# Differential attention: the first turn of a unit between the halves of its second scores, and six value tiles in front of them instead of three

## The chip, the cores and the metric

One core of a Trainium2 chip runs the whole kernel. The metric is the time of one execution on the device in microseconds; of the kernel before, three runs and one profiled execution are known. The clock of TensorE (PE) is told as granted clock, 1.00 being 2.4 GHz and 0.50 being 1.2 GHz.

## What is computed

The reference is two blocks of a model over 2048 positions with 1024 channels, in float32. The change concerns one part of the first block, the differential attention with 4 heads. Each head has two sets of queries and keys (64 wide) and one set of values (128 wide):

```python
def block(args):
    qblk, qp = args
    s = jnp.einsum('bqhce,bkhce->bchqk', qblk, k).astype(jnp.float32) * scale
    dist = jnp.abs(qp[:, None] - pos[None, :]).astype(jnp.float32)
    s = s - slopes[:, None, None] * dist
    a = jax.nn.softmax(s, axis=-1)
    w = a[:, 0] - lam * a[:, 1]
    return jnp.einsum('bhqk,bkhe->bqhe', w.astype(v.dtype), v)
```

## The kernel before, in words

The stage `diff_attention` works through 64 units, 4 heads by 16 tiles of 128 queries. A unit's scores against all 2048 keys are made twice (set s = 0 and s = 1), turned into weights, mixed, transposed ("turned") and multiplied with the values. Everything is held in order by semaphores, and each engine's instructions stand in an order written out by hand, one loop over m for each engine. The waits are placed as `wait_ge` in front of an instruction, and an engine does not pass over a waiting instruction.

Names used below, with what each waits for:

- S00, S01, S10, S11 are the calls `scores(m + 2, s, half)` of PE (L2033), s first, half second. Each fills two of the four banks `score` with 1024 keys: three passes of two matmuls. Half 0 has banks 0 and 1, half 1 banks 2 and 3. A call waits until DVE has read the scores that its banks held before (`score_read[half]`), so S11 waits for B01 of the same unit, and S10 for B00.
- B00, B01, B10, B11 are `bias_and_top(m + 2, s, half)` of DVE (L1974): they add the distance term, write the result into `e` and keep the running minimum (`half_top`, then `neg_top`). B01 and B11 are over when the accumulator has been read.
- E0 and E1 are `exp(m + 2, s)` of ACT (L1894). E0 needs B01's minimum, E1 needs B11's. Both leave a sum.
- The reciprocal (L1984, `invert_total(m + 1)`) needs the sum of E1 of the turn before. The mix (L1994, `mix(m + 1)`) combines both sets of weights.
- T0 and T1 are `transposes(m, group)` of PE (L2044), 16 small matmuls each, into the two banks `turn`. T0 needs the mix of unit m and, like T1, that ACT has moved what the banks held before.
- Moves are `move(m, r)` of ACT (L1902), two for each turn, from `turn` to `w_t`.
- V-first and V-rest are `values(m - 1, first, last)` of PE (L2061): 16 value tiles of 128 keys, each with 2 calls, which the trace shows as 4 matmuls. V-first is tiles 0 to EARLY - 1, V-rest is EARLY to 15. They add into the two banks `out`, which have no second buffer; V-first waits for `a_copied`, that is for C of the unit before (m - 2). V-rest tells `valued` at its end.
- C is `copy_out(m - 2)` of ACT (L1909): it needs `valued` of unit m - 2 and moves `out` to `a_parts`. POOL adds the two parts (L1851), ACT squares the sum (L1916), and SP stores it (L1818).

The order of one turn of the loop, for m in the middle, on each engine:

```
PE   S00 S01 V-first T0 S10 S11 V-rest T1
DVE  B00 reciprocal B01 B10 weigh B11 mix
ACT  C, moves of T1 (unit m-1), moves of T0 (unit m), E0, square, E1
```

POOL also makes the high and low parts of later queries and keys, and pieces of a bias table for the stage behind; SP loads queries, keys and values. Neither is touched.

Of the kernel before, what the change touches and what calls it, by code (L numbers as in the profile page):

```python
# [1694 lines left out]
def diff_attention(nc, c, inputs, wait_z_stored, lambdas, cols, rows, a_rows, a_sums, a_squares, bias):  # L1695
# [7 lines left out]
    UNITS = DIFF_HEADS * NT  # L1703

    with Phase(nc, "d") as ph:
# [52 lines left out]
        def wait_q_made(eng, n):  # L1758

            if n == 0:  # L1760
                eng.wait_ge(q_first_made, 1)
            else:
                eng.wait_ge(q_made, n)

        def wait_k_made(eng, h, s):

            if h == 0:
                eng.wait_ge(k_first_made, s + 1)
            else:
                eng.wait_ge(k_made, 2 * h)  # L1770

        EARLY = 3
        FILLED_AT = (11, 12, 15)

        def quad_of(m):

            return m // 4

        def wait_mixed(eng, m, group):

            if group == 0:
                eng.wait_ge(mixed, m + 1)

        def wait_turn_free(eng, m, group):

            if 2 * m + group >= 1:
                eng.wait_ge(moved, 4 * m + 2 * group)

        def wait_group_moved(eng, m, group):

            eng.wait_ge(moved, 4 * m + 2 * group + 2)

        @block.sync
        def _(sp):
            def load_v(h):
                at = (DV + h) * P
                sp.dma_start(v[:, h % 2], rows[:, at:at + VW].rearrange("(t p) n -> p t n", p=P))\
                  .then_inc(v_loaded[h % 2], 16)

            for n, vec in enumerate(lambdas):  # L1800
                sp.dma_start(lam_in[:, n], row_on_all(vec, P)).then_inc(lam_loaded, 16)
            load_v(0)
            load_v(1)
            wait_z_stored(sp)
            bias.load_first(sp, cols)
            for m in range(UNITS):
                h, t = m // NT, m % NT
                if m % 4 == 0 and quad_of(m) + 2 < DIFF_HEADS * QUADS:
                    wait_q_made(sp, quad_of(m))
                    inputs.load_q(sp, quad_of(m) + 2)  # L1810
                if t == 1 and h + 1 < DIFF_HEADS:
                    wait_k_made(sp, h, 1)
                    inputs.load_k(sp, h + 1)
                if t == 3 and 1 <= h and h + 1 < DIFF_HEADS:
                    sp.wait_ge(valued, NT * h)
                    load_v(h + 1)
                sp.wait_ge(a_added, m + 1)
                sp.dma_start(a_rows[t * P:(t + 1) * P, h * VW:(h + 1) * VW], a_out[:, m % 4]).then_inc(a_stored[m % 4], 16)  # L1818
            for s in range(4):
                sp.wait_ge(a_stored[s], 16 * UNITS // 4)  # L1820
# [197 lines left out]
        @block.tensor  # L2018
        def _(pe):
            def scores(m, s, half):  # L2020
                h, n = m // NT, quad_of(m)
                if m % 4 == 0 and s == 0 and half == 0:
                    wait_q_made(pe, n)
                if m % NT == 0 and half == 0:
                    wait_k_made(pe, h, s)
                if 2 * m + s >= 1:
                    pe.wait_ge(score_read[half], 2 * m + s)
                queries = slice((m % 4) * P, (m % 4 + 1) * P)
                keys = slice(half * BANK, (half + 1) * BANK)
                for n_pass, (q_part, k_part) in enumerate(((q_hi, k_hi), (q_hi, k_lo), (q_lo, k_hi))):  # L2030
                    for b in range(2):
                        at = slice(b * HD, (b + 1) * HD)
                        mm = pe.matmul(score[:, 2 * half + b], q_part[at, n % 2, s, queries], k_part[at, h % 2, s, keys],  # L2033
                                       start=(n_pass == 0), stop=(n_pass == 2))
                mm.then_inc(scored, 1)

            def transposes(m, group):
                wait_mixed(pe, m, group)
                wait_turn_free(pe, m, group)
                for b in range(8):  # L2040
                    kt = 8 * group + b
                    for side in range(2):
                        at = slice(side * HD, (side + 1) * HD)
                        mm = pe.transpose(turn[:, side, b * HD:(b + 1) * HD], e[at, m % 3, 0, kt * P:(kt + 1) * P],  # L2044
                                          ident[at, at])
                mm.then_inc(turned, 1)

            def values(m, first, last):
                h = m // NT
                if first == 0:  # L2050
                    if m % NT == 0:
                        pe.wait_ge(v_loaded[h % 2], 16 * (h // 2 + 1))
                    if m >= 1:
                        pe.wait_ge(a_copied, m)
                    wait_group_moved(pe, m, 0)
                for kt in range(first, last):
                    if kt == 8:
                        wait_group_moved(pe, m, 1)
                    for side in range(2):
                        at = slice(side * HD, (side + 1) * HD)  # L2060
                        mm = pe.matmul(out[:, side, 0:VW], w_t[at, m % 2, kt], v[at, h % 2, kt], start=(kt == 0),  # L2061
                                       stop=(kt == NT - 1))
                if last == NT:
                    mm.then_inc(valued, 1)

            for m in range(-2, UNITS + 1):
                if m + 2 < UNITS:
                    scores(m + 2, 0, 0)
                    scores(m + 2, 0, 1)
                if m >= 1:  # L2070
                    values(m - 1, 0, EARLY)
                if 0 <= m < UNITS:
                    transposes(m, 0)
                if m + 2 < UNITS:
                    scores(m + 2, 1, 0)
                    scores(m + 2, 1, 1)
                if m >= 1:
                    values(m - 1, EARLY, NT)
                if 0 <= m < UNITS:
                    transposes(m, 1)  # L2080
# [1672 lines left out]
def build(nc, a, choice, result):  # L3753
# [14 lines left out]
    with Phase(nc, "k") as ph:  # L3768
# [14 lines left out]
        with Phase(nc, "b") as held:  # L3783
            bias = DilatedBias(held, c["carry"])
            diff_attention(nc, c, diff_inputs, wait_z_stored, [a[f"lambda_{n}"] for n in ("q1", "k1", "q2", "k2")], cols, rows, a_rows, a_sums,
                           a_squares, bias)
            dilated_attention(nc, c, cols, rows, o_parts, bias, w_merge, a_sums, a_squares, root)
            held.clear()
# [35 lines left out]
```

## Time and profile before

| | |
|---|---|
| median of 3 runs | 2932.22 us (2930.03 to 2933.57) |
| profiled execution | 2932.87 us, its span 2931.0 us, mean granted clock 0.972 |
| busy share of the span | PE 93%, DVE 70%, ACT 53%, POOL 36% |
| the stage | scores from 766.4 us, last values from 1295.3 us |
| one turn of its loop | 8.05 us |

The page gives the busy time of each engine, waits with the instruction that ended them ("<-"), and groups of instructions by line. A matmul's length in the trace is partly modelled and overlaps with the next, so PE's cost is read from start to start. "x12" means that twelve instructions of one kind in a row are merged into one line, and the number in front is then the length of them all.

### The profile page before, as it was taken

How to read it: one execution, taken by the hardware profiler on the slowest of the kernel's cores; microseconds unless marked ns; L12 is line 12 of the kernel's file. 1: busy time of each engine (PE TensorE's matmuls, PEld its weight loads, DVE VectorE, ACT ScalarE, POOL GpSimd, SP SyncE). 2: the span in 40 equal slices, each digit the busy share in tenths (PEclk: the TensorE clock that was granted, in tenths of full speed). 3: DMA queues.
4: the chain of work that ended last, by engine and by line, in shares of the span. 5: the costliest groups of instructions: out<-in, count | busy, mean ns of one | idle time of the engine just before them, and what ended most of it. 6: DMA issues, size and time to landing. Idle time of an engine off the chain costs nothing. (4 is left out here: it accounts for less than half of the span.)

```text
span 2931.0 us, 54522 instructions
## 1 busy us (share of the span) xinstructions
PE 2731.9 (93%) x21026; PEld 2233.1 (76%) x21026; DVE 2045.2 (70%) x3027; ACT 1559.6 (53%) x3111; POOL 1053.4 (36%) x803
## 2 busy tenths in 40 slices
PE   7899989999699999989998899899899999799998
PEld 5678867888588888878887678688677788577776
DVE  5767687666799999967777765433567767466675
ACT  6574446644588888867776221322433343455553
POOL 4677656776122222129550543200021111221211
PEclk9999999999899999999999899899999999899999
DMA  3433323332412121023443666242165465744441
GB/s 115 129 108 94 94 80 93 108 108 87 133 24 54 32 53 25 24 63 114 119 119 109 235 217 252 85 145 79 51 181 132 98 158 161 177 148 135 144 155 67
DMA packets 317438, 330.11 MB, mean 113 GB/s; under 512 B 24401, under 2 KB 259969, under 8 KB 314113
## 3 DMA queue, kind: packets, MB, share of 16 engines
q1 hardware_dynamic: 287184, 292.59, 32.8%
q0 software_dynamic: 6912, 23.07, 2.7%
q10 hardware_dynamic: 23088, 11.02, 1.6%
q8 instruction: 166, 2.72, 0.4%
q14 instruction: 88, 0.71, 0.1%
HBM read 217.13 MB, written 109.47 MB: 111 GB/s over the span
## 5 line engine op out<-in xcount | busy, mean ns | idle before, releaser
L1049 PE MATMUL p_acc<-p_y_hi,p_x_hi 128*128 128x512 f32 x904 | 362.2, 401 | 11.4 <-DVE p_y_lo L841 3.8
L1049 PE MATMUL p_acc<-p_y_lo,p_x_hi 128*128 128x512 f32 x904 | 356.4, 394 | 0.0
L1049 PE MATMUL p_acc<-p_y_hi,p_x_lo 128*128 128x512 f32 x904 | 356.1, 394 | 0.0
L562 POOL TENSOR_TENSOR p_x_lo<-k_carry,p_x_hi 128x1024 fp32r<-128x1024 f32 x113 | 281.1, 2494 | 131.9 <-ACT p_x_hi L634 131.9
L1894 ACT ACTIVATE d_e<-d_e,d_neg_top 128x2048 f32<-128x2048 f32 x128 | 256.9, 2007 | 18.9 <-DVE d_neg_top L1974 18.9
L2061 PEld LDWEIGHTS d_out<-d_v,d_w_t 64*128 64x128 f32 x4096 | 248.0, 188 | 11.9 <-ACT d_a_parts L1909 0.8
L920 DVE RECIPROCAL p_aux<-p_aux 128x512 f32<-128x512 f32 x64 | 215.1, 3361 | 57.5 <-ACT p_aux L730 57.5
L2061 PE MATMUL d_out<-d_v,d_w_t 64*128 64x128 f32 x4096 | 249.7, 272 | 0.7 <-ACT d_a_parts L1909 0.7
L1565 PE MATMUL s_acc<-s_y_hi,s_x_hi 128*128 128x512 f32 x560 | 224.1, 400 | 22.0 <-DVE s_x_lo L1369 12.9
L1565 PE MATMUL s_acc<-s_y_lo,s_x_hi 128*128 128x512 f32 x560 | 221.5, 395 | 0.0
L1565 PE MATMUL s_acc<-s_y_hi,s_x_lo 128*128 128x512 f32 x560 | 221.1, 395 | 0.0
L1049 PEld LDWEIGHTS p_acc<-p_y_hi,p_x_hi 128*128 128x128 f32 x904 | 172.3, 191 | 50.5 <-issue 9.3
L2327 ACT ACTIVATE l_e<-l_score,l_stage 128x256 f32<-128x256 f32 (+1 forms) x384 | 163.1, 438 | 86.6 <-DVE l_stage L2368 86.5
L1049 PEld LDWEIGHTS p_acc<-p_y_hi,p_x_lo 128*128 128x128 f32 x904 | 171.8, 190 | 37.8
L1049 PEld LDWEIGHTS p_acc<-p_y_lo,p_x_hi 128*128 128x128 f32 x904 | 172.0, 190 | 34.8
L1851 POOL TENSOR_TENSOR d_a_out<-d_a_parts 128x128 f32<-128x128 f32 x64 | 29.5, 460 | 412.7 <-ACT d_a_parts L1909 372.8
L1974 DVE CUSTOM_DVE_ANT_0 d_e<-d_score,d_dist 128x1024 f32<-128x1024 f32 x128 | 156.5, 1222 | 29.6 <-PE d_score L2033 29.6
L1902 ACT ACTIVATE d_w_t<-d_turn 128x512 f32<-128x512 f32 x256 | 138.1, 593 | 68.7 <-PE d_turn L2044 68.5
L1974 DVE CUSTOM_DVE_ANT_0 d_e<-d_score,d_dist,d_half_top 128x1024 f32<-128x1024 f32 x128 | 164.4, 1284 | 6.4
L243 POOL DMA_DIRECT2D k_carry<-in_a_w_in x72 | 53.8, 752 | 311.7 <-DVE s_x_lo L1369 311.3
L3577 DVE CUSTOM_DVE_ANT_0 w_e_in<-w_score,k_carry,w_less 128x256 f32<-128x256 f32 (+1 forms) x256 | 111.4, 473 | 73.0 <-PE w_score L3674 72.3
L634 ACT ACTIVATE p_x_hi<-k_carry 128x1024 fp32r<-128x1024 f32 x113 | 119.2, 1056 | 80.1 <-PE p_acc L1049 56.0
(367 smaller groups left out, 7097.6 us busy)
## 6 DMA issues: line engine op xcount, KB each, us to landing
k_carry<-in_w_in SPq DMA_DIRECT2D x128, 256.0 KB, 3.3
k_carry<-in_a_w_in POOLq DMA_DIRECT2D x72, 256.0 KB, 3.6
cols<-p_z SPq DMA_DIRECT2D x64, 256.0 KB, 2.6
w_q<-q SPq DMA_DIRECT2D x15, 1024.0 KB, 8.2
o_parts<-l_stage SPq DMA_DIRECT2D x192, 66.0 KB, 1.8
m_o<-o_parts SPq DMA_DIRECT2D x48, 264.0 KB, 5.9
k_carry<-cols SPq DMA_DIRECT2D x48, 256.0 KB, 4.7
j_x_second<-x SPq DMA_DIRECT2D x20, 512.0 KB, 3.8
```

The source lines that it names most:

```text
L243: sp.dma_start(self.w_raw[:, j, k_half, c_half], self.w_b[block][:, k_half, c_half]).then_inc(arrived, 16)
L562: pool.tensor_tensor(x_lo[:, m % RING], inputs.place(x_place(m)), x_hi[:, m % RING].bitcast(F32), ALU.subtract).then_inc(x_lo_made, 1)
L634: act.activation(x_hi[:, m % RING], inputs.place(place), ACT.Copy).then_inc(x_hi_made, 1)
L920: dve.reciprocal(norm_bank(m), norm_bank(m)).then_inc(root_inverted, 1)
L1049: mm = pe.matmul(bank_of(n, j), x_part[:, n % RING, j, kt], y_part[:, y_slot(n), kt], start=(kt == 0 and m == 0 and not (g == 0 and n % 2 ...
L1565: mm = pe.matmul(bank_of(n, j), x_part[:, n % RING, j, kt], y_part[:, form, kt], start=(kt == 0 and m == 0), stop=(kt == 3 and m == 2))
L1894: act.activation(e[:, m % 3, s], e[:, m % 3, s], ACT.Exp, bias=neg_top[:, m % 2, s:s + 1], scale=-1.0, accum_out=sums).then_inc(exped, 1)
L1902: act.activation(w_t[:, m % 2, 8 * group:8 * group + 8, side * HD:(side + 1) * HD], turn[:, side].rearrange("p (b n) -> p b n", n=HD), ACT ...
L1974: dve.tensor_tensor_reduce(e[:, m % 3, s, half * HALF:(half + 1) * HALF], score[:, 2 * half:2 * half + 2].rearrange("p a b -> p (a b)"), d ...
L2061: mm = pe.matmul(out[:, side, 0:VW], w_t[at, m % 2, kt], v[at, h % 2, kt], start=(kt == 0), stop=(kt == NT - 1))
L2327: act.activation(e[:, u % 4, h, 0:width(n)], score[:, 2 * (n % 2) + h, scores_of(n, j)], ACT.Exp, bias=stage[:, u % SLOTS, 2 * HD + h:2 * ...
L3577: dve.tensor_tensor_reduce(e_in[:, h, at], score[:, s % 2, j * WIN + at.start:(j + 1) * WIN], tables[:, h, at], -1.0, less[:, h:h + 1], AL ...
```

## The change

V-first takes six value tiles (24 matmuls in the trace) where it took three (12), V-rest takes ten (40) where it took thirteen (52), and T0 stands behind S10 where it stood in front of it. S10 and S11 with T0 between them are the halves of the second scores. The other engines' orders, all waits and all buffers stay. PE's order becomes S00 S01 V-first S10 T0 S11 V-rest T1. In turns without scores (the last three) or without values (the first ones) the calls that exist keep this order.

```diff
-        EARLY = 3
+        EARLY = 6
...
                     scores(m + 2, 0, 1)
                 if m >= 1:
                     values(m - 1, 0, EARLY)
+                if m + 2 < UNITS:
+                    scores(m + 2, 1, 0)
                 if 0 <= m < UNITS:
                     transposes(m, 0)
                 if m + 2 < UNITS:
-                    scores(m + 2, 1, 0)
                     scores(m + 2, 1, 1)
                 if m >= 1:
                     values(m - 1, EARLY, NT)
```

## Rows read from the trace of the kernel before

**Rows 1.** Busy time by engine in one stretch of the stage, with the granted clock

```profile
1100.00:1200.00 100.00, 96.05 (x1510) 85.54 (x1508) 93.12 (x138) 84.11 (x137) 25.13 (x34) 1.00 0.11 26
```

**Rows 2.** Who waited for whom, from 1000 to 1250 us: total, times, longest

```profile
ACT d_w_t L1902 <- PE d_turn L2044: 33.6, 31, 1.1
...
DVE d_e L1974 <- PE d_score L2033: 15.2, 32, 0.5
PE d_score L2033 <- DVE d_neg_top L1974: 10.2, 31, 0.3
```

**Rows 3.** PE in order of time over one turn of the loop: start, length, count

```profile
1207.33 0.66 PE L2044 MATMUL d_turn<-k_ident,d_e 64*128 64x64 f32 x16
1207.79 0.48 PE L2033 MATMUL d_score<-d_k_hi,d_q_hi 64*128 64x512 f32 x2
...
1208.58 0.39 PE L2033 MATMUL d_score<-d_k_hi,d_q_hi 64*128 64x512 f32 x2
...
1209.27 0.83 PE L2061 MATMUL d_out<-d_v,d_w_t 64*128 64x128 f32 x12
1209.93 0.66 PE L2044 MATMUL d_turn<-k_ident,d_e 64*128 64x64 f32 x16
1210.40 0.47 PE L2033 MATMUL d_score<-d_k_hi,d_q_hi 64*128 64x512 f32 x2
...
1211.67 0.50 PE L2033 MATMUL d_score<-d_k_hi,d_q_hi 64*128 64x512 f32 x2 [0.33 <-DVE d_neg_top L1974]
...
1212.47 3.06 PE L2061 MATMUL d_out<-d_v,d_w_t 64*128 64x128 f32 x52
1215.37 0.66 PE L2044 MATMUL d_turn<-k_ident,d_e 64*128 64x64 f32 x16
```

**Rows 4.** DVE in order of time over the same turn

```profile
1208.92 1.22 DVE L1974 CUSTOM_DVE_ANT_0 d_e<-d_score,d_dist 128x1024 f32<-128x1024 f32 x1 [0.48 <-PE d_score L2033]
...
1211.53 1.22 DVE L1974 CUSTOM_DVE_ANT_0 d_e<-d_score,d_dist 128x1024 f32<-128x1024 f32 x1
...
1214.15 2.35 DVE L1994 SCALAR_TENSOR_TENSOR d_e<-d_e,d_ratio 128x2048 f32<-128x2048 f32 x1
1216.97 1.23 DVE L1974 CUSTOM_DVE_ANT_0 d_e<-d_score,d_dist 128x1024 f32<-128x1024 f32 x1 [0.47 <-PE d_score L2033]
```

**Rows 5.** ACT in order of time over the same turn

```profile
1208.21 0.36 ACT L1909 ACTIVATE d_a_parts<-d_out 128x256 f32<-128x256 f32 x1
1208.47 1.07 ACT L1902 ACTIVATE d_w_t<-d_turn 128x512 f32<-128x512 f32 x2
1210.63 1.09 ACT L1902 ACTIVATE d_w_t<-d_turn 128x512 f32<-128x512 f32 x2 [1.09 <-PE d_turn L2044]
1211.65 2.01 ACT L1894 ACTIVATE d_e<-d_e,d_neg_top 128x2048 f32<-128x2048 f32 x1
...
1214.26 2.01 ACT L1894 ACTIVATE d_e<-d_e,d_neg_top 128x2048 f32<-128x2048 f32 x1 [0.22 <-DVE d_neg_top L1974]
...
1216.27 0.36 ACT L1909 ACTIVATE d_a_parts<-d_out 128x256 f32<-128x256 f32 x1
```

**Rows 6.** All engines at the end of the stage, in order of time

```profile
1280.67 0.36 ACT L1909 ACTIVATE d_a_parts<-d_out 128x256 f32<-128x256 f32 x1
...
1281.08 0.75 PEld L2061 LDWEIGHTS d_out<-d_v,d_w_t 64*128 64x128 f32 x12 [0.79 <-ACT d_a_parts L1909]
1281.08 0.94 PE L2061 MATMUL d_out<-d_v,d_w_t 64*128 64x128 f32 x12 [0.65 <-ACT d_a_parts L1909]
...
1288.32 1.09 ACT L1902 ACTIVATE d_w_t<-d_turn 128x512 f32<-128x512 f32 x2 [0.89 <-PE d_turn L2044]
1289.29 0.31 ACT L1916 ACTIVATE d_unused<-d_a_out 128x128 f32<-128x128 f32 x1
```

**Rows 7.** Stretches of 4 us at the stage's start: busy times and granted clock

```profile
776.00:780.00 4.00, 2.35 (x16) 0.97 (x12) 3.97 (x8) 2.10 (x2) 0.00 (x0) 1.00 1.08 386
...
784.00:788.00 4.00, 4.00 (x34) 2.48 (x32) 3.58 (x6) 2.40 (x3) 0.00 (x0) 0.66 0.26 56
```

## The prediction

> **What bounds the kernel now.** The change touches one stage, so I read that stage alone. The busy times come first [rows 1]: in 100 us of it PE is busy 96.05, DVE 93.12, ACT 84.11, at a granted clock of 1.00, which is 2.4 GHz. No engine is full, so a loop of waits sets the pace, not one engine's work. The waits [rows 2] say which: in 250 us PE waits 31 times for the minimum that DVE leaves (the score banks come free with it), DVE waits 32 times for PE's scores, ACT waits 31 times for a turn. 250 us hold 31 units, so each happens once per unit.
>
> Then the order in time. PE [rows 3]: T1 starts at 1207.33 and again at 1215.37; DVE repeats after 8.05 us, 1208.92 to 1216.97 [rows 4], which I take as the turn. Between, from start to start: S00 0.79 (1207.79 to 1208.58), S01 0.69, V-first with its 12 matmuls 0.66, T0 0.47, S10 1.27 (1210.40 to 1211.67), S11 0.80, V-rest with 52 matmuls 2.90, T1 0.46. S00 shows what S10 costs without a wait, 0.79; so 0.48 us are lost at S11. Its releaser is B01 on DVE, which is over when B10 starts, at 1211.53 [rows 4].
>
> So the loop of before is: S00 starts at 1207.79; B00 at 1208.92, 1.13 later; B00, reciprocal and B01 end at 1211.53; S11 starts at 1211.67; S11, V-rest and T1 take 0.80 + 2.90 + 0.46, and S00 follows. 1.13 + 2.61 + 0.14 + 4.16 = 8.04. DVE has 0.48 us idle in it [rows 4], and so could go at 8.05 - 0.48 = 7.57; PE's own work is also 8.05 - 0.48 = 7.57.
>
> ACT is the engine to look at next [rows 5]. C starts at 1208.21, the two moves of T1 at 1208.47, then ACT stands idle 1.09 us for T0; moves of T0 1210.63, E0 1211.65, the square, then 0.22 us idle for B11's minimum, E1 1214.26, C 1216.27. PE had ended that unit's V-rest by 1207.33, where T1 starts [rows 3], yet C waits until E1 gives ACT free: ACT works in the order that is written, and C stands behind E1 of the turn before. V-first needs C (the `out` banks have no second buffer). In before C to V-first is 1208.21 to 1209.27, which is enough.
>
> **The change, part by part.** Nothing is added or removed: 16 value tiles, two turns and four score calls per unit remain, no DMA is moved; SP's stores follow C by way of POOL's sum, once per unit, as they do now.
>
> (1) What it does for the loop of before. Six value tiles leave V-rest for V-first (3 tiles, 12 matmuls), and T0 goes from before S10 to before S11. A matmul of V-rest takes 2.90 / 52 = 0.0558 us [rows 3], so V-rest falls to 40 x 0.0558 = 2.23. The old loop becomes 1.13 + 2.61 + 0.14 + 0.80 + 2.23 + 0.46 = 7.37: it no longer binds, and S11's wait goes, because S11 is now 0.79 + 0.69 + 1.34 + 0.79 + 0.47 = 4.08 behind S00's start where B01's result is there after 3.88. The 0.48 are off. Without anything else, PE and DVE would both go at 7.57.
>
> (2) What it does to T0. T0 stands 0.79 + 0.69 + 0.66 = 2.14 behind S00's start now; with 12 more value matmuls (0.67) and S10 (0.79) before it, 3.60. So ACT's moves of T0 come 1.46 later against PE's beginning of the turn. Behind them on ACT stand E0, the square, E1 and C, and for C waits PE's V-first, and behind V-first stand S10 and T0. That is a closed loop, PE to ACT to PE, one turn long:
> C's start to V-first's start 0.41, from the last turns of the stage, where V-first does wait for C (1280.67 to 1281.08) [rows 6];
> V-first, 24 x 0.0558 = 1.34, and 0.11 for starting after a wait: 12 matmuls show 0.94 there [rows 6] against 0.83 in the stream [rows 3]; 1.45 together;
> S10 up to T0, 0.79 as after a turn, since scores behind value matmuls stand nowhere in this stage. The lower end is S01 behind S00, 0.69 [rows 3]; I take 0.79, since the kind of matmul changes here as it does behind a turn;
> T0 to the first move 0.70 (1209.93 to 1210.63) [rows 3, 5];
> the two moves up to the next ACT instruction 0.97 (1288.32 to 1289.29) [rows 6];
> E0 to E1: 1211.65 to 1214.26 is 2.61, of which 0.22 are the wait for B11 and 0.09 the overlap that two ACT instructions have (C's 0.36 against 0.26 to the move behind it shows 0.10): 2.30 [rows 5];
> E1 to C 2.01 (1214.26 to 1216.27) [rows 5].
> Sum: 0.41 + 1.45 + 0.79 + 0.70 + 0.97 + 2.30 + 2.01 = 8.63 us.
>
> The same loop in before, with V-first 0.66 and no S10 in it, is 0.41 + 0.66 + 0.70 + 0.97 + 2.30 + 2.01 = 7.05, a full microsecond below 8.05; that is why it shows nowhere now. It will be the longest: 8.63 against 8.05.
>
> (3) Do the other waits hold? Take V-first's start as 0. S10 starts at 1.45, T0 2.24, S11 2.71, V-rest 3.50, T1 5.73, next S00 6.19, S01 6.98, V-first could go at 7.67 and waits until 8.63, some 0.96. DVE: S10 started at 1.45 frees B10 at 1.45 + 1.13 = 2.58, where DVE was free at about 1.5; so DVE, too, gets a new wait of 1.1 us, at B10, while that at B00 goes (mix ends at 7.5, behind S00 + 1.13 = 7.32). B11 ends near 5.2; E1, which needs it, comes at 1.45 + 0.79 + 0.70 + 0.97 + 2.30 = 6.21, so ACT's 0.22 go. E0 at 3.91 has its minimum long before. T0's banks are free when T1's moves end, 1.35 behind C's start [rows 5], that is at 0.94. The reciprocal needs E1's sum, there at about C's start plus 0.1, -0.3, and comes at about 0. All are covered, the last by 0.3 us alone, and there a miss costs nothing below 1 us, as B10 waits anyway. POOL's sum and casts, at 25 us busy in 100 [rows 1], lie beside this.
>
> (4) How often. Turns 2 to 62 of the loop start V-first behind a C, and 60 steps lie between them, all with an E0 and E1 in them. 60 x (8.63 - 8.05) = 34.8. The few turns at the start (without values) and at the end (without scores) have other orders; I leave both at 0, within 1.5 us either way.
>
> The profiled execution took 2932.87 us round a span of 2931.0, the three runs 2932.22 in the median, 0.65 less. 2932.87 + 34.8 = 2967.7 for it, and 2967.0 for the median.
>
> **A rule weighed.** The weight load of V-first after C starts together with its matmul, at 1281.08, and shows a wait of its own for C, 0.79 us [rows 6]; so nothing of V-first is prepared during the wait. The Trainium skill, TensorE: Matmul & The Clock Gate, section "Architectural detail: the array is 16× 32×32, not 1× 128×128", says that PE's queue can take a weight load ahead of matmuls in flight. By that rule the 0.11 for the restart would not arise, the loop would be 8.52 and the time 2960; by the row it is 8.63 and 2967. I go by the row, since it is this very wait.
>
> **The rivals.**
> (a) Faster. The wait for C never comes late, because ACT has room for the late T0; then DVE sets the pace at 7.57, 60 x 0.48 = 28.8 less, 2903. For it: S11's wait does go, and ACT is busy 84 of 100 us only. Against: the room that ACT has between S00 and C can be counted. V-first starts 1.06 behind C where 0.41 would do, 0.65; E1's wait with the overlap 0.31; 0.05 at E0 (1.02 against 0.97). That is 1.01, and T0 comes 1.46 later, 1.57 with the restart. It decides at a loop sum of 8.05: below it the change gains. It takes a sum wrong by 0.58.
> (b) No difference: the same with a room near 1.5. The gain in S11 and the loss at V-first would have to cancel within 6 us of 2932, 0.1 us per turn.
> (c) Slower still, by the clock. PE will stand idle about 1 us per 8.6, not 0.48 per 8.05. At the stage's start PE was busy 2.35 of 4 us at clock 1.00, and one stretch later the mean is 0.66, so 1.2 GHz for most of it [rows 7]. Were it at 1.2 GHz throughout, V-first, S10 and T0 in the loop would lose about their 1.34 + 0.7 again, 2.0 us per turn, 120 in all; for a quarter of the turns 30, 2997. Against: PE remains busy some 88 in 100, and nothing of the kind shows at 96 [rows 1] nor do I expect it well above the 59 in 100 that went before the fall.
> (d) DVE's new wait at B10 sets the pace in ACT's place: S10 to B10 1.13, B10 to mix's end 4.97 (1211.53 to 1214.15, and 2.35) [rows 4], B00 1.15, its release 0.14, S10 again: 7.4, below 8.63. Then it would be faster than before too; I count it with (a).
>
> **How the numbers follow.** Forecast 86 in 100; (a) with (d) 5, (b) 3, (c) 6. In the forecast's own case: low, S10 at 0.69 and no restart, 8.42, 60 x 0.37 = 22, 2954; high, S10 0.10 dearer than taken and E0 to E1 without the overlap, 2.39, with 1.5 for the ends, 8.82, 60 x 0.77 + 1.5 = 48, 2980. I set 2953 to 2979; this holds nine tenths of the case, some 8 in 10 of all, and reaches to neither rival, as both lie beyond what is left out. 0.2% of 2932, 6 us, is about what this measurement can tell: faster 5, the same 3, slower 92.
>
> **What would show it.** In the changed profile: T1 to T1 near 8.63; PE's wait of S11 for DVE gone and one of V-first for ACT's copy in its place, 60 times, near 1 us; DVE's wait moved to B10, 1.1 us; ACT's idle before T0's moves near 2.1 instead of 1.09, and none before E1; clock 1.00. If no wait of V-first for the copy shows, the forecast is wrong at step (2); if it shows and the turn is not near 8.6, a price is.

## The result, and the profile after

The changed kernel takes 2960.06 us (median of 4 runs, 2957.57 to 2961.23) against 2931.64 of the kernel before (4 runs); the ratio is 1.0096, with a 95% interval of 1.0085 to 1.0108. It is slower by 28 us. The profiled execution took 2960.39 us round a span of 2958.5 us, 27.5 more than that of before, at the same mean clock of 0.972.

The busy times of one stretch, in the columns of [rows 1]:

```profile
1100.00:1200.00 100.00, 90.47 (x1410) 80.12 (x1407) 88.55 (x131) 78.68 (x132) 26.94 (x35) 1.00 0.09 25
```

All three engines of the loop are less busy than in [rows 1], PE 90.47 for 96.05, and the clock is 1.00 as before: no engine got more work, the turn got longer. The waits of the same 250 us as in [rows 2]:

```profile
ACT d_w_t L1902 <- PE d_turn L2044: 55.6, 29, 2.0
PEld d_out L2061 <- ACT d_a_parts L1909: 33.0, 27, 1.2
DVE d_e L1974 <- PE d_score L2033: 27.1, 29, 1.0
PE d_out L2061 <- ACT d_a_parts L1909: 21.3, 27, 0.8
```

PE's wait for DVE's minimum is gone from the list. In its place V-first waits for ACT's copy C, 27 times here and two more for which no releaser is named. PE over one turn, as in [rows 3]:

```profile
1207.99 1.61 PE L2061 MATMUL d_out<-d_v,d_w_t 64*128 64x128 f32 x24 [0.79 <-ACT d_a_parts L1909]
...
1209.36 0.48 PE L2033 MATMUL d_score<-d_k_hi,d_q_hi 64*128 64x512 f32 x2
...
1210.13 0.66 PE L2044 MATMUL d_turn<-k_ident,d_e 64*128 64x64 f32 x16
...
1210.59 0.48 PE L2033 MATMUL d_score<-d_k_hi,d_q_hi 64*128 64x512 f32 x2
...
1211.37 2.40 PE L2061 MATMUL d_out<-d_v,d_w_t 64*128 64x128 f32 x40
...
1215.30 0.40 PE L2033 MATMUL d_score<-d_k_hi,d_q_lo 64*128 64x512 f32 x2
...
1216.50 1.61 PE L2061 MATMUL d_out<-d_v,d_w_t 64*128 64x128 f32 x24 [0.80 <-ACT d_a_parts L1909]
```

ACT over the same turn, as in [rows 5]:

```profile
1207.57 0.38 ACT L1909 ACTIVATE d_a_parts<-d_out 128x256 f32<-128x256 f32 x1
...
1210.84 1.09 ACT L1902 ACTIVATE d_w_t<-d_turn 128x512 f32<-128x512 f32 x2 [1.92 <-PE d_turn L2044]
...
1211.81 2.01 ACT L1894 ACTIVATE d_e<-d_e,d_neg_top 128x2048 f32<-128x2048 f32 x1
...
1214.09 2.00 ACT L1894 ACTIVATE d_e<-d_e,d_neg_top 128x2048 f32<-128x2048 f32 x1
...
1216.07 0.38 ACT L1909 ACTIVATE d_a_parts<-d_out 128x256 f32<-128x256 f32 x1
```

Read the two together as one ring, which is the closed loop of the prediction, one turn long: C 1207.57, V-first 1207.99, S10 1209.36, T0 1210.13, moves 1210.84, E0 1211.81, E1 1214.09, C 1216.07, V-first 1216.50. No instruction in it waits for anything outside it: 0.42 from C's start to V-first's, then each leg from start to start, 0.42 + 1.37 + 0.77 + 0.71 + 0.97 + 2.28 + 1.98 = 8.50. Between, PE reaches V-first too early: the last scores start at 1215.30, V-first could follow 0.23 later, and starts at 1216.50, 0.97 late. DVE waits in another place than in [rows 4], at B10 instead of B00:

```profile
1210.45 1.22 DVE L1974 CUSTOM_DVE_ANT_0 d_e<-d_score,d_dist 128x1024 f32<-128x1024 f32 x1 [0.94 <-PE d_score L2033]
```

V-first of the second turn of the loop starts at 799.71 us, before at 798.72; that of turn 62 at 1310.04, before at 1281.08 [rows 6]. So 1.0 us come from the start, 28.0 from the 60 turns: 8.505 a turn for 8.039. From turn 62's V-first to the last C it is 13.63 us for 14.52, 0.9 less, and what follows the stage is 0.6 shorter in this profile, which leaves the 27.5.

### The profile page after: what moved, and what is told of

The parts are those of the page before. It is cut to its first block and busy times, and to the rows that moved or that the text cites. A ratio compares the mean times of both kernels' runs of the same rounds, so it can differ in the third digit from the quotient of the medians.

```text
span 2958.5 us, 54522 instructions
## 1 busy us (share of the span) xinstructions
PE 2733.0 (92%) x21026; PEld 2237.8 (76%) x21026; DVE 2044.1 (69%) x3027; ACT 1550.4 (52%) x3111; POOL 1054.5 (36%) x803
## 5 line engine op out<-in xcount | busy, mean ns | idle before, releaser
L2061 PE MATMUL d_out<-d_v,d_w_t 64*128 64x128 f32 x4096 | 256.7, 275 | 49.1 <-ACT d_a_parts L1909 46.6
```

## The experiments

All were timed against the kernel before on the same chip: 2931.68 us for the first four, 2929.46 for the last four. Turns are C to C in each trace, a mean over three to six turns near 1200 us.

### Order alone, tiles alone

`order_only` is the changed kernel with

```diff
-        EARLY = 6
+        EARLY = 3
```

> Only the order of the change: T0 behind S10, V-first still 3 value tiles. Theory of the loop through C (C, V-first, S10, T0, moves, E0, square, E1, C): it sums to 0.42 + 0.70 + 0.77 + 0.71 + 0.97 + 2.28 + 1.98 = 7.83 us, below the 8.04 of the old loop over S11, so the time stays at that of before, 2932, within 3 us, and PE waits for C at V-first not at all or by less than 0.2. Rival, the late place of T0 is by itself what costs: most of the 28 us here, 2950 to 2960.

Measured: 2933.89 us, ratio 1.0002 (0.9993 to 1.0011): no difference. A turn is 8.05. V-first's weight load shows a small wait for C:

```profile
PEld d_out L2061 <- ACT d_a_parts L1909: 9.6, 29, 0.4
```

The matmuls themselves start only 0.05 us later for it (1211.87, where the last scores start at 1211.59 and the stream's step is 0.23). So the late T0 by itself costs nothing that the runs can tell; the rival's 2950 to 2960 is out.

`tiles_only` is the kernel before with

```diff
-        EARLY = 3
+        EARLY = 6
```

> Only the tiles of the change: six in V-first, ten in V-rest, T0 in front of S10 as before. Theory of the loop through C: over T0 it sums to 0.42 + 1.37 + 0.71 + 0.97 + 2.28 + 1.98 = 7.73; but there is a second way round, V-first, T0, S10, B10, B11, E1, C: 1.37 + 0.47 + 1.13 + 2.62 + 0.12 + 1.98 + 0.42 = 8.11, so the turn is 8.11 and the time 2936, with a wait for C at V-first of some 0.6 us in every turn all the same. Rival, six tiles in front are by themselves what costs: 2950 to 2960.

Measured: 2940.20 us, ratio 1.0029 (1.0018 to 1.0041), 8.5 us more; a turn is 8.16. V-first waits in each turn:

```profile
1213.40 1.61 PE L2061 MATMUL d_out<-d_v,d_w_t 64*128 64x128 f32 x24 [0.43 <-ACT d_a_parts L1909]
1214.84 0.66 PE L2044 MATMUL d_turn<-k_ident,d_e 64*128 64x64 f32 x16
```

and E1 waits 0.24 us for B11, as the second way round says:

```profile
1210.98 2.01 ACT L1894 ACTIVATE d_e<-d_e,d_neg_top 128x2048 f32<-128x2048 f32 x1 [0.24 <-DVE d_neg_top L1974]
```

The ring over B10 and B11 was expected at 8.11 and is 8.16. The expectation took 1.37 for V-first, as in the changed kernel, where S10 stands behind it; here T0 does, and starts 1.44 behind V-first (1213.40 to 1214.84). By the starts of this trace the ring is V-first 1.44, T0 0.47, S10 up to B10 1.10, B10 and B11 2.61, up to E1 0.12, E1 2.01, C 0.41: 8.16.

The order alone gives nothing that can be told, the tiles alone 8 us, the whole 28: they do not add. The ring over T0, the moves and E0 had about 1 us of room before the change (7.05 against 8.05 in the prediction). The order puts 0.77 into it, which fits, and the tiles 0.67 more, which does not. With the tiles alone that ring has room left, and the one over B10 and B11 binds.

### C out of the ring

`copy_before_e1` is the changed kernel with ACT's copy of a unit moved in front of E1 of the turn in which its V-rest is made:

```diff
             for m in range(-2, UNITS + 2):
-                if m >= 2:
-                    copy_out(m - 2)
                 if 0 <= m - 1 < UNITS:
...
                 if m >= 2:
                     square_out(m - 2)
+                if 1 <= m <= UNITS:
+                    copy_out(m - 1)
                 if m + 2 < UNITS:
                     exp(m + 2, 1)
```

> The changed kernel, with C of a unit issued on ACT between the square and E1 of the same turn in which its V-rest is made, instead of behind E1. Theory of the loop through C: E1 (1.98 us) is out of the loop, V-first no longer waits, and DVE's own work sets the pace, 7.57 us a turn: 2932 - 60 x 0.47 = 2904. Rival one, the late T0 costs because E0 and E1 come late for DVE's reciprocal: E1 now comes later by 0.26 more, so 2960 or more. Rival two, the late S10 costs by DVE's wait at B10, whatever C does: 2960, B10's wait stays at 0.94.

Measured: 2897.66 us, ratio 0.9886 (0.9871 to 0.9901), 34 us below the kernel before and 62 below the changed one. A turn is 7.48. In a steady turn neither V-first nor DVE waits any more; over the 250 us of [rows 2] V-first waits once, 0.2 us, T0 once, 1.4 us, and DVE once, 1.0 us, where the changed kernel shows a wait of V-first and one of DVE in every turn. The engines stand so (PE, PEld, DVE, ACT, POOL, clock):

```profile
1000.00:1250.00 250.00, 248.37 (x3998) 228.24 (x3995) 245.64 (x367) 219.48 (x368) 79.39 (x74) 1.00 0.14 34
```

T0 and S10 stand here as late in PE's order as in the changed kernel, and E1 even later on ACT. Both rivals said 2960 or more. What costs 28 us in the change is V-first's wait for a C that stands behind E1; with this wait gone, the new order gives what it has to give, the removal of S11's wait.

The turn is 0.09 below the 7.57 that the prediction gave for DVE and for PE. On DVE the mix is followed by B00 without a wait, 2.26 from start to start (1207.29 to 1209.55), where the mix's length of 2.35 was reckoned. On PE, V-first, which waits for nothing here, takes 1.25 up to S10, where 24 x 0.0558 = 1.34 was reckoned:

```profile
1209.77 1.51 PE L2061 MATMUL d_out<-d_v,d_w_t 64*128 64x128 f32 x24
1211.02 0.49 PE L2033 MATMUL d_score<-d_k_hi,d_q_hi 64*128 64x512 f32 x2
```

B10 starts at 1212.16, when B01's result has been read, and 1.14 behind S10's start, which is what it needs from S10 as well. So DVE and PE both go at very nearly their own work here, and the trace does not tell which of them sets the 7.48.

`copy_on_before` makes the same move of C in the kernel before:

> The kernel before with C between the square and E1, as in copy_before_e1. Theory: C and all behind it on ACT now wait for V-rest, which has 13 tiles and ends late here: end of V-rest to C 0.29, C 0.26, E1 2.00, T1's moves and their release 1.13, T0 0.47, S10 0.79, S11 0.69, V-rest 2.90 = 8.53 a turn, 2932 + 29 = 2961. Rival, C in front of E1 is simply the better place, whatever PE's order: 2932 or less.

Measured: 2967.01 us, ratio 1.0116 (1.0099 to 1.0133), 38 us more; a turn is 8.59. C waits for V-rest, and T0 for the moves that stand behind E1:

```profile
1210.83 0.39 ACT L1909 ACTIVATE d_a_parts<-d_out 128x256 f32<-128x256 f32 x1 [0.99 <-PE d_out L2061]
...
1214.32 0.71 PE L2044 MATMUL d_turn<-k_ident,d_e 64*128 64x64 f32 x16 [0.92 <-ACT d_w_t L1902]
```

The turn is 0.06 above the expected 8.53, and the time 6 us above the expected 2961. Part of this lies in the last turns: the last four C take 18.4 us from first to last (1313.87 to 1332.30), 14.9 in before (1280.67 to 1295.60), which the expectation left out.

So the early C is no better place in itself. It needs a V-rest that is over in time, and that is what the six tiles in front make.

### One piece of ACT's part of the ring

`square_in_gap` is the changed kernel with the square in ACT's idle time:

```diff
+                if m >= 2:
+                    square_out(m - 2)
                 if 0 <= m < UNITS:
                     move(m, 0)
                     move(m, 1)
                 if m + 2 < UNITS:
                     exp(m + 2, 0)
-                if m >= 2:
-                    square_out(m - 2)
```

> The changed kernel, with ACT's square moved from between E0 and E1 into the idle time in front of T0's moves. Theory of the loop through C: ACT's chain from T0 to C loses 0.29 us, the turn falls from 8.51 to 8.22, the time from 2960 to 2943. Rival, DVE's wait at B10 or PE's order sets the pace: no change, 2960.

Measured: 2944.09 us, ratio to before 1.0041 (1.0028 to 1.0055), 16 us below the changed kernel; a turn is 8.21. One ACT instruction of 0.3 us, moved past idle time of its own engine, is worth 0.30 a turn. ACT is 79 in 100 busy before this step and 80 after it (1100 to 1200 us).

### The dose

How does the turn follow the number of value tiles in V-first? Three more sizes of V-first: `new_order_4` and `new_order_8` are the changed kernel with EARLY = 4 and 8, `old_order_4` is the kernel before with EARLY = 4.

> The changed order with four value tiles in V-first. Theory of the loop through C: 0.42 + 0.92 + 0.77 + 0.71 + 0.97 + 2.28 + 1.98 = 8.05 us a turn, as long as the turn of before: the time is that of before, 2931 to 2935. Rival, every tile moved costs the same: one third of 28 us, 2941.

> The changed order with eight value tiles in V-first. Theory of the loop through C: each tile adds 4 x 0.0558 = 0.22 us to the loop, 8.51 + 0.45 = 8.96 a turn, the time 2960 + 27 = 2987, and V-first's wait for C grows by the 0.45. Rival, PE only does the same work in another place and something fixed costs the 28 us: 2960.

> The kernel before with four value tiles in V-first and T0 where it was. The old loop over S11 loses one tile: 8.04 - 0.22 = 7.82; the way round over V-first, T0, S10, B10, B11, E1 and C is 0.92 + 0.47 + 1.13 + 2.62 + 0.12 + 1.98 + 0.42 = 7.66. So 7.82 a turn and 60 x 0.22 = 13 us less: 2918. Rival, the time of tiles_only lies on a line with that of before: one third of its 8 us more, 2935.

| kernel | time, us | ratio to before (95%) | turn, us | expected turn |
|---|---|---|---|---|
| new order, 3 tiles | 2933.89 | 1.0002 (0.9993 to 1.0011) | 8.05 | 8.04 |
| new order, 4 | 2934.65 | 1.0016 (1.0006 to 1.0025) | 8.06 | 8.05 |
| new order, 6 (the change) | 2960.06 | 1.0096 (1.0085 to 1.0108) | 8.51 | 8.63 |
| new order, 8 | 2990.42 | 1.0191 (1.0171 to 1.0212) | 8.95 | 8.96 |
| old order, 4 | 2918.62 | 0.9952 (0.9936 to 0.9969) | 7.83 | 7.82 |
| old order, 6 | 2940.20 | 1.0029 (1.0018 to 1.0041) | 8.16 | 8.11 |

In the new order the turn rises by 0.22 a tile from four tiles on, and not at all from three to four: a bend where one ring takes over from another, as expected, and no line through the points. In the old order the time is lower at four tiles (the ring over S11 is shorter by one) and higher at six (the ring over B10, B11 and C binds); five were not run. That three tiles to six make a small loss there hides a gain of 11 us at four. `new_order_4` is 5 us above the before of its chip, where at most 3 were expected, with a turn only 0.01 longer than that of before; its profiled span is 2931.3, like before's 2931.0. Where those few microseconds arise, the traces do not show; it stays open.

## Why the prediction was right, point by point

**What bounds.** The ring over S11 and its 0.48 us: gone in the trace of after, and worth the 0.2 us a tile in `old_order_4`.

**Step (1)**, S11's wait goes: right; no such wait is in the list.

**Step (2)**, the ring through C: right as a mechanism; `copy_before_e1`, `square_in_gap` and the dose each show it from another side. Its sum was 8.63 and the turn is 8.51, so the forecast, 2967.0, lies 7 us above the measured 2960.06. The step that was mis-sized is mostly the term for V-first: 1.45 was taken, 1.37 measured (1207.99 to 1209.36). Its two parts can be told apart by runs. The restart, 0.11, was right: 24 value matmuls with S10 behind them take 1.36 after a wait (median from 1000 to 1240 us in after) and 1.25 without one (`copy_before_e1`), from start to start. The stream price was not: the 0.0558 came from V-rest, behind which a turn follows, and a turn starts later behind value matmuls than scores do. After a wait the same 24 matmuls take 1.44 up to T0 (`tiles_only`, and in after the last turns, which have no scores: 1310.04 to 1311.48), nearly what 1.34 and 0.11 give, and 1.36 up to S10. With scores behind it V-first is 0.08 cheaper. The prediction had said that no row shows scores behind value matmuls; it looked for that price in S10, and it lies in V-first.

The other legs: C to V-first 0.42 for 0.41, S10 0.77 for 0.79, T0 to the moves 0.71 for 0.70, the moves 0.97 for 0.97, E0 to E1 2.28 for 2.30, E1 to C 1.98 for 2.01; together 0.05 less. S10 behind value matmuls costs what it does behind a turn, as was chosen.

**Step (3)**, the other waits: V-first's wait 0.96, measured 0.97 by starts; DVE's at B10 1.1, measured 0.94; ACT's before T0's moves 2.1, measured 1.92; none before E1, none found.

**Step (4)**, 60 turns: 60 x 0.466 = 28.0 and 1.0 more at the start, 0.9 less at the end; both were left at 0 within 1.5.

**The rule weighed.** By the rule of the Trainium skill, TensorE: Matmul & The Clock Gate, section "Architectural detail: the array is 16× 32×32, not 1× 128×128", the sum came to 8.52 and 2960, which is the measured time. Its mechanism is not what the trace shows across the wait: the weight load of V-first starts with its matmul here too, and waits longer than it, as this row of the weight loads says.

```profile
1207.99 1.42 PEld L2061 LDWEIGHTS d_out<-d_v,d_w_t 64*128 64x128 f32 x24 [1.22 <-ACT d_a_parts L1909]
```

Where V-first waits for nothing, in `copy_before_e1`, its weight load starts 0.22 us ahead of its matmul (1209.55 and 1209.77), so there the trace agrees with the rule. The restart of 0.11 does arise, as the row said. The number of the rule was right by luck: it left out 0.11 that are there, and V-first before scores is 0.08 cheaper for another reason.

**The rivals.** (a) with (d), faster: out; the ring takes 8.51, and the change would have gained only below 8.05. It is, though, what happens when C is taken out of the ring, at 2898. (b), no difference: out for the change, but `order_only` is that case: its room holds 0.77, not 0.77 and 0.67. (c), the clock: 1.00 in the stretch of after as in [rows 1], with PE 90 in 100 busy; it did not fall there. Two readings of (c) were off: between its two stretches lies a third (780 to 784, PE busy 2.08 of 4 us, clock 0.91), and V-first, S10 and T0 are 1.34 + 0.79 + 0.47 = 2.6 us, not 2.0.

## What to carry to other kernels

When an instruction is moved back on one engine, follow what the next engine does behind it in its own written order, up to where that order comes back to the first engine, and add up the ring from start to start. Two edits, of which one costs nothing and the other 8 us, can cost 28 together when they lengthen one ring, and the way to use them is then a third edit elsewhere: here the copy of `out` in front of the second exponential turns 28 us lost into 34 gained. An engine that is idle a fifth of the time can hold most of the ring that sets the pace; move a small instruction of it into its own idle time, and the turn tells.

## What was not expected of the hardware

What a group of matmuls costs from start to start depends on what stands on either side of it. The 24 value matmuls of V-first take 1.25 us up to scores when they wait for nothing, 1.36 when they start after a wait, and 1.44 after a wait when a turn stands behind them. Their length in the trace shows the wait (1.50 without, 1.61 with) but not the neighbour behind: it is 1.61 up to scores and up to a turn alike. A ring wants starts, taken from a row with the same neighbours.

At the stage's start S10 now stands alone behind a wait of 2.44 us, and the granted clock is at 0.50 over the whole of 784 to 788, where it was 0.66 [rows 7], and at 0.71 in the next four microseconds, where it was 1.00 in before:

```profile
784.00:788.00 4.00, 3.94 (x32) 2.93 (x34) 2.79 (x7) 1.40 (x3) 0.00 (x0) 0.50 0.34 68
788.00:792.00 4.00, 4.00 (x50) 3.58 (x50) 3.91 (x4) 4.00 (x5) 0.00 (x0) 0.71 0.01 2
```

The order of the first turns lets PE stand idle for longer in one piece before it, and the scores behind cost 1.43 to 1.44 us at 1.2 GHz where they cost 0.8 at 2.4. PE was idle for 2.44 us just before; in before, 1.30 and 0.43 us with a turn between them. That this is the 1.0 us by which the second turn is late was not tried by itself.
